# One contiguous token range per core, each with its own branch of the program

## The reference

```python
u = rmsnorm(h, ln1_g); z = u @ w_in       # -> zb, zc, zv (1024 each), q_lat 768, kv_lat 512, k_rope 64, gates 4096
y_conv = (zb * causal_dwconv3(zc * zv, conv_w)) @ w_conv_out
q = (rmsnorm(q_lat) @ w_q_b)              # 16 heads of 192
kv = (rmsnorm(kv_lat) @ w_kv_b)           # 16 heads of 128 (k) + 128 (v)
# per head: RMS norm of q and k over 192, rotary on the last 64, causal softmax(q k^T / sqrt(192)) v
y_mla = attention @ w_mla_out
h = h + (sigmoid(gate_a) * y_conv + sigmoid(gate_b) * y_mla) @ w_o
u = rmsnorm(h, ln2_g)
a = causal_dwconv3(u @ w_ffn_up, ffn_conv_w) + ffn_conv_b          # 2 * 5632 wide
h = h + (silu(a_gate) * a_up) @ w_ffn_down
```

## Time and profile before

| | us |
|---|---|
| median of 3 runs | 2585.52 |
| lowest, highest | 2583.54, 2963.02 |
| span of the profiled execution (slowest core, 0) | 2586.2 |
| spans of the 8 cores | 2577.1 to 2586.2 |
| PE busy | 2530.2 |
| DVE busy | 1483.1 |
| ACT busy | 1031.8 |
| POOL busy | 184.1 |
| HBM read | 320.30 MB |

### The profile page before, as it was taken

How to read it: one execution, slowest core, us unless ns; L and a number is a source line. 1 busy time by engine, 2 the same in 40 slices (tenths; PEclk the granted TensorE clock), 3 DMA queues, 4 the chain that set the end, 5 groups by cost and what they waited for, 6 DMA issues and landing times.

```text
span 2586.2 us, 51956 instructions; the slowest of 8 cores (2577.1 to 2586.2 us)
## 1 busy us (share of the span) xinstructions
PE 2530.2 (98%) x18360; PEld 1640.8 (63%) x18360; DVE 1483.1 (57%) x3020; ACT 1031.8 (40%) x2044; POOL 184.1 (7%) x321
## 2 busy tenths in 40 slices
PE   4999999999999999999999999999999999999999
PEld 2887666666666666666666666666556646666544
DVE  3881788787877878751211122377547736777611
ACT  4883688888888888841111113300000000000000
POOL 1010000000000000000000000010111010111010
PEclk9999999999999999999999999999999999999999
DMA  9684111202020102334444466344444454444465
GB/s 195 165 140 76 23 37 23 43 19 48 14 49 21 40 13 44 105 78 78 70 81 72 73 142 146 67 75 78 68 82 74 70 82 79 74 75 75 85 131 118
DMA packets 64779, 195.69 MB, mean 76 GB/s; under 512 B 7248, under 2 KB 8784, under 8 KB 63440
## 3 DMA queue, kind: packets, MB, share of 16 engines
q0 software_dynamic: 45648, 144.33, 34.1%
q1 hardware_dynamic: 18880, 48.03, 5.9%
HBM read 320.30 MB, written 15.83 MB: 130 GB/s over the span
## 4 chain that ended last, share of the span: by engine, by line
PE 95%; DMA 2%; DVE 2%; issue 1%; ACT 1%; SPq 0%; DVEq 0%; POOL 0%; ACTq 0%; POOLq 0%
PE ps L516 95%; DMA arena<-wkvin 1%; DVE arena L530 1%; DVE arena L534 1%; ACT arena L523 1%; DMA arena<-xg 1%; SPq L550 0%; DVE arena L540 0%; DVEq L200 0%; DVE arena L547 0%; POOL arena L550 0%; ACTq L200 0%; POOLq L200 0%; SPq L200 0%
## 5 line engine op out<-in xcount | busy, mean ns | idle before, releaser
L516 PE MATMUL ps<-arena 128*128 128x390 bf16 (+9 forms) x18360 | 2530.2, 300 | 53.2 <-ACT arena L523 25.1
L516 PEld LDWEIGHTS ps<-arena 128*128 128x128 bf16 x18360 | 1640.8, 98 | 942.3 <-issue 82.5
L534 DVE TENSOR_TENSOR arena<-ps,arena 128x390 f32<-128x390 f32 (+6 forms) x713 | 353.8, 502 | 812.7 <-PE ps L516 787.2
L534 DVE TENSOR_TENSOR arena<-arena 128x130 bf16<-128x130 bf16 (+18 forms) x1522 | 663.7, 474 | 231.8 <-ACT arena L523 204.3
L523 ACT ACTIVATE arena<-ps,arena 128x260 bf16<-128x260 f32 (+7 forms) x992 | 518.9, 546 | 419.0 <-PE ps L516 363.3
L523 ACT ACTIVATE arena<-arena 128x390 bf16<-128x390 f32 (+14 forms) x412 | 269.0, 677 | 844.6 <-DVE arena L530 725.3
L530 DVE SCALAR_TENSOR_TENSOR arena<-arena 128x1024 f32<-128x1024 f32 (+9 forms) x499 | 371.7, 762 | 37.1 <-ACT arena L523 13.1
L523 ACT ACTIVATE arena<-ps 128x512 bf16<-128x512 f32 (+11 forms) x635 | 319.8, 524 | 112.9 <-PE ps L516 107.1
L550 POOL DMA_DIRECT2D arena<-wall x286 | 167.1, 585 | 2235.5 <-PE ps L516 2181.8
L543 DVE TENSOR_SCALAR arena<-arena 128x1024 f32<-128x1024 f32 (+1 forms) x90 | 72.3, 803 | 0.0
L530 DVE SCALAR_TENSOR_TENSOR arena<-ps,arena 128x256 bf16<-128x256 f32 (+1 forms) x80 | 33.2, 464 | 6.7 <-ACT arena L523 4.1
(11 more groups left out here) (3 smaller groups left out, 0.3 us busy)
## 6 DMA issues: line engine op xcount, KB each, us to landing
arena<-wall POOLq DMA_DIRECT2D x182, 512.0 KB, 5.3
arena<-wall POOLq DMA_DIRECT2D x64, 352.0 KB, 4.7
arena<-xg POOLq DMA_DIRECT2D x22, 512.0 KB, 11.0
arena<-xo SPq DMA_DIRECT2D x16, 520.0 KB, 24.2
arena<-xg SPq DMA_DIRECT2D x8, 1024.0 KB, 6.5
arena<-wall POOLq DMA_DIRECT2D x32, 256.0 KB, 5.0
outT<-arena SPq DMA_DIRECT2D x31, 256.0 KB, 3.4
arena<-wkvin SPq DMA_DIRECT2D x16, 320.0 KB, 16.3
```

The source lines that it names most:

```text
L516: S.add(PE, lambda e: e.matmul(out, lhsT=lhsT, rhs=rhs, start=start, stop=stop), reads, writes, cost=max(width(rhs) / 2400.0, 0.055) + 0.003)
L534: S.add(DVE, lambda e: e.tensor_tensor(out=out, in0=in0, in1=in1, op=op), reads, writes, cost=dcost(out, in0, in1) + held)
```

## The change

Core j of a batch element owns one contiguous range of tokens, `BOUNDS` = 0, 1238, 2304, 3246, 4096. The program now has four bodies, one per range, made by `share_program(Share(j), ...)`; each engine reads `which` from DRAM and takes its body in one of four `If`s. A body handles keys only up to its range's end (`nkb` = 10, 18, 26, 32 key blocks). It has `na` = n + 2 columns in chunks of at most 510 (3 chunks on the first two ranges, 2 on the others). Each range's queries are cut in chunks of at most 512 (3, 3, 2, 2), each chunk's key blocks begin at the column where the block becomes visible, and one PSUM bank (4 or 5) holds a chunk's result; the mask is one triangle of 128 columns. Six `PT` buffers instead of four, `LA` 4 instead of 2, four `acc`. `b0_units`, `halo`, `halo2` go; the halo tokens come with the block that holds them. In the first stage own blocks may be both of a group; on range 0 the first two groups are own blocks that come as bf16 for `latents` and again as f32, late, for `own`. Attention and conv results are loaded for the mix ahead of the last score only where they lie under the rotary keys. `up` does both weights per chunk and its conv steps per chunk; the FFN's down groups are 10, 10, 10, 7, 7 tiles instead of 4 x 11, and its last groups use chunks `O` of at most 512.

```diff
+BOUNDS = (0, 1238, 2304, 3246, 4096)
+class Share:
+    def __init__(self, j):
+        self.s, self.e = BOUNDS[j], BOUNDS[j + 1]
+        self.n = self.e - self.s
+        self.na, self.nu = self.n + 2, self.n + 4
+        self.t0 = self.s - 2
+        self.h0 = 2 if self.first else 0
+        self.nkb = 2 * ((self.e + 255) // 256)
+        self.nkh = (self.e + 127) // 128
+        self.k = 128 * self.nkb
+        self.T = split(self.na, 510)
+        self.chunks = [(self.h0 + o, self.h0 + o + n) for o, n in split(self.na - self.h0, 512)]
+        self.O = split(self.n, 512)
...
+def emit(nc, which, progs):
...
+    def body(e, eng):
+        v = eng.value_load(which[0:1, 0:1])
+        for j, (S, final_waits) in enumerate(progs):
+            with eng.If(v == j):
+                S.replay(e, eng, eng_sem, chan_sem, final_waits)
...
     def oload(i, behind=()):
-        dma(SP, xo_[i % 3].rearrange("p k n -> p (k n)"), xg[i * 512:i * 512 + 128, :], ...)
+        b = sh.own[i][0]
+        dma(SP, xo_[i % 3].rearrange("p k n -> p (k n)"), xg[b * 128:b * 128 + 128, :], ...)
...
     def own(i):
+        b, g, h, _ = sh.own[i]
+        lo, hi = max(128 * b, sh.s - 4, 0), min(128 * b + 128, sh.e)
+        o = lo - (sh.s - 4)
+        x0, n = lo - 128 * b, hi - lo
         for k in range(16):
-            stt(u_own[:, k, o:o + 128], xo_[i % 3][:, k, :], C("g1", k), rstdx[:, y, 0:128], ALU.mult, ALU.mult,
+            stt(u_own[:, k, o:o + n], xo_[i % 3][:, k, x0:x0 + n], C("g1", k), rstdx[:, y, 128 * h + x0:128 * h + x0 + n],
+                ALU.mult, ALU.mult,
...
+    for h in range(NH):
+        for ci, (c0, c1) in enumerate(sh.chunks):
+            kbs = [kb for kb in range(sh.nkh) if 128 * kb <= sh.t0 + c1 - 1]
+            cs = h * len(sh.chunks) + ci
+            span[cs] = (len(pieces), len(pieces) + len(kbs))
+            for kb in kbs:
+                pieces.append((cs, h, kb, max(c0, 128 * kb - sh.t0), c0, c1))
...
-    NPT = 4
-    PT, TPT = P4.slabs(NPT, [912], BF16, "PT")
-    acc, Tacc = P4.slabs(2, [912], F32, "acc")
+    NPT = 6
+    PT, TPT = P4.slabs(NPT, [sh.CW], BF16, "PT")
+    acc, Tacc = P4.slabs(4, [sh.CW], F32, "acc")
...
+    def pv(i):
+        cs, h, kb, a, c0, c1 = pieces[i]
+        b = 4 + cs % 2
+        mm(PS[b][:, a - c0:c1 - c0], Vh[hb][:, kb, :], PT[:, x, a - c0:c1 - c0], i == span[cs][0], i == span[cs][1] - 1,
...
-                if (tag, i) in mixed or Tsrc[i].w is None or (tag == "gc" and i == 7 and st_s.units):
+                if (tag, i) in mixed or Tsrc[i].w is None or (st_s.units and t[i].hi > kro):
...
     def up(j):
+        for t, (off, n) in enumerate(T3):
+            for gi, key, A__, y_, Ty_, jc in ((0, "fg", Ag, yg, Tyg, j), (1, "fu", Au, yu, Tyu, 44 + j)):
+                for k in range(16):
+                    mm(PS[p][:, 0:n], w[:, k, :], u2[:, k, off:off + n], k == 0, k == 15, [Tw, Tu2[k]], [TP[p]])
+                tt(A__[:, off:off + n], PS[p][:, 0:n], rstd2[:, t, 0:n], ALU.mult, ...)
+                ts(y, A__[:, lo + 2:lo + 2 + m], C("fcw", 3 * jc + 2), C("fcb", jc), ALU.mult, ALU.add, rd, [Ty_[x]])
+                stt(y, A__[:, lo + 1:lo + 1 + m], C("fcw", 3 * jc + 1), y, ALU.mult, ALU.add, ...)
+                stt(y, A__[:, lo:lo + m], C("fcw", 3 * jc + 0), y, ALU.mult, ALU.add, ...)
```

More of the change, by code:

```diff
@@ new lines, in emit, with _ @@
+def emit(nc, which, progs):
+    for S, _ in progs:
+        S.finalize()
+    eng_sem = {e: nc.alloc_semaphore("sem_" + e) for e in ENGS}
+    chans = []
+    for S, _ in progs:
+        chans += [c for c in S.chan_cnt if c not in chans]
+    chan_sem = {c: nc.alloc_semaphore("dsem_" + str(c)) for c in chans}
+    def body(e, eng):
[3 more added lines that the diff above has]
+                S.replay(e, eng, eng_sem, chan_sem, final_waits)
+    with nc.Block() as block:
+        @block.tensor
+        def _(eng):
+            body(PE, eng)
+        @block.scalar
+        def _(eng):
+            body(ACT, eng)
+        @block.vector
+        def _(eng):
+            body(DVE, eng)
+        @block.gpsimd
+        def _(eng):
+            body(POOL, eng)
+        @block.sync
+        def _(eng):
+            body(SP, eng)
@@ L359, with split @@
+def split(n, most):
+    k = -(-n // most)
+    w = 2 * (-(-n // (2 * k)))
+    out, o = [], 0
+    while o < n:
+        out.append((o, min(w, n - o)))
+        o += w
+    return out
 QSCALE = 192.0 ** -0.5
 KB = 1024
-ARENA = 208896
+ARENA = 212800
 _c = {}
@@ L371 @@
 NC_CONST = _o
-T3 = [(0, 390), (390, 390), (780, 260)]
-T3C = [(0, 390), (390, 390), (780, 276)]
-HALF = 456
+FG = (10, 10, 10, 7, 7)
+FO = tuple(sum(FG[:g]) for g in range(6))
+NFT = 14
 def weight_plan():
@@ L984, in build_program, with ownof, loaded @@
+    def ownof(g):
+        return max([i for i, o in enumerate(sh.own) if o[1] == g] + [-1])
+    def loaded(g, h):
+        return at("cast") >= mode[(g, h)] if (g, h) in mode else at("ld%d" % g) > 0
+    rlast, rprior = {}, {}
+    for g in range(NG):
+        rprior[g] = ownof(rlast[rslab[g]]) if rslab[g] in rlast else -1
+        rlast[rslab[g]] = g
+    for g in range(NG):
         if g == 1:
@@ new lines, in plain, with sums @@
+    def plain(cs):
+        a, b = span[cs]
+        return b - a >= 4 and all(pieces[a + m][3] == pieces[a + m][4] for m in range(4))
+    def sums(i):
+        cs, h, kb, a, c0, c1 = pieces[i]
+        x, m = i % NPT, i - span[cs][0]
+        n = c1 - c0
+        A = a - c0
+        y = 2 * (cs % 2)
+        xp = (i - 1) % NPT
+        if plain(cs):
+            if m < 4:
+                if m % 2:
+                    z = y + m // 2
+                    tt(acc[:, z, 0:n], PT[:, xp, 0:n], PT[:, x, 0:n], ALU.add, [TPT[xp], TPT[x]], [Tacc[z]])
+                return
+            z = y + m % 2
+            tt(acc[:, z, A:n], acc[:, z, A:n], PT[:, x, A:n], ALU.add, [Tacc[z], TPT[x]], [Tacc[z]])
+        elif m == 0:
+            cp(acc[:, y, 0:n], PT[:, x, 0:n], [TPT[x]], [Tacc[y]])
+        else:
+            tt(acc[:, y, A:n], acc[:, y, A:n], PT[:, x, A:n], ALU.add, [Tacc[y], TPT[x]], [Tacc[y]])
```

975 lines of the change are left out of this document (448 added, 527 removed).

## The result

The changed kernel takes 2486.74 us (median, 2485.44 to 2486.83); against the kernel before the ratio is 0.9618, with a 95% interval of 0.9601 to 0.9635. It is 3.8% faster; the forecast of 2444 us meant 5.5%.

What follows compares the result with a forecast made beforehand. PE's columns bound the kernel; slowest type 0: start 143 + heads 543.0 + 24.7 + behind them 1694.0 + 29.5 + tail 2.8 = 2437.0, plus branches 8: span 2445, median 2444 us; range 2400 to 2500, its own 2428 to 2464.

Steps and rivals of the forecast that it cites:

- Bound and columns: Whole kernel: PE's columns set the time; they fall from 2448.7 us to 2264.7 to 2284.0, a gain of 165 to 182.
- Start of type 0: First stage, first range: ends at 143 us (120 to 155), set by DVE's own products and a chain of buffer reloads.
- The rival at 20%, start hidden: First stage, type 0: own blocks done by 100 to 120 us, type 1 or 0 last at 2400 to 2425; 20%.
- the q latents read it whole: First stage: it ends only when every own block is in `u_own`, since the query latents read all of it.
- Feed-forward part costed at nothing: Feed-forward: three short conv steps per chunk replace one of 1024; fixed costs add a fifth at most, charged 0 us.
- Branches: Reading `which` and testing it four times, leaping over up to three foreign programs: 8 us, between 0 and 25.
- Four at about 2: Branches: four leaps at about 2 us each, nearest to the shortest DMA landing of 1.7 us, making the 8 us.
- the upper bound of 25: Branches: one register read and four leaps at 5 us, three times the shortest DMA landing, 25 us at most.
- Losses in the heads: Head stage: 6.2 ns lost per matmul beside the columns, 24.7, 37.2, 38.2 and 45.4 us on types 0 to 3.
- Head chain on type 3: Head stage: rival that pieces form a dependent chain and type 3 is last, 2498 to 2546, mild form 2450 to 2500; 14%.
- Code loading: Whole program: rival that instruction blocks aren't fetched ahead after a leap, 269 us for 251 packets, giving 2713 us; 3%.
- Weights and mix loads at nothing: Weight DMAs (share 0.48 to 0.59 on type 3) and later mix loads stay covered: 0 us, mix at most 14.

Runs made afterwards that it cites:

- own_nogain: Changed kernel with each own block's 16 products made one product over all slabs, gain g1 left out; 2472.13 us in one execution.
- ffn_wide: Changed kernel with feed-forward taps, silu and product run once over the whole range again, first multiply still per chunk; 2469.83 us, ratio 0.9546.
- ffn_inter: Changed kernel with gate and up convolution steps taking turns on DVE, each chunk's product issued behind the next chunk's first two products; 2469.52 us, ratio 0.9543.
- before_chunked: Kernel before, with only the feed-forward convolution, silu and product run per chunk of one PSUM bank; 2668.65 us, ratio 1.0312.
- nested_rev: Changed kernel with branches as an if/else-if chain, type 3 tested first, type 0 last; types 0 to 3 ended at 2486.0, 2480.2, 2396.2, 2400.3 us (cores 4-7).
- one_type1: Changed kernel holding only type 1's body, without branch or type read, run by all eight cores; median span 2469.7 us.

## Why the prediction was right or wrong

**Bound and columns: right.** PE's columns set the time; the stage columns came out as counted, and the matmuls but for 14 behind the heads. The columns fell by 165 to 184 us (the prediction's own sums give 184 for type 3, not 182). On types 2 and 3 they fell by 180 and 184, and the spans by 187 and 169.

**Start of type 0: right mechanism, and the number partly by luck.** Forecast 143, measured 142.2 (137.1 on core 4), with PE idle ahead of it and DVE as its last releaser; own_nogain shows the chain. The rival at 20%, start hidden, falls. But the steps differ from those forecast. DVE's products on type 0, the first, the fifth block and the last three blocks (start, us):

```profile
71.05 0.34 DVE L599 SCALAR_TENSOR_TENSOR arena<-arena 128x128 bf16<-128x128 f32 x1
...
116.88 2.71 DVE L599 SCALAR_TENSOR_TENSOR arena<-arena 128x128 bf16<-128x128 f32 x10 [5.18 <-ACT arena L592]
...
133.34 13.58 DVE L599 SCALAR_TENSOR_TENSOR arena<-arena 128x128 bf16<-128x128 f32 x50 [2.17 <-DMA arena<-xg]
```

They began at 71, not 80; `own(4)` began at 116.9 for 118; the last block ran from 141.8 to 146 us and not from 138 to 143. PE started at 142.2 all the same, because the first query latent matmul needs only the first slab of that block: "the q latents read it whole" was wrong as a condition for the start. An early first step, slower reloads and an early PE cancelled out. What the forecast didn't see either is the landing of head weights, 11.4 us of PE's wait on type 0 and 7.0 on type 1: hidden by the own chain on the one, while on the other it makes 7.0 of the +9.3 in the heads.

**Feed-forward part costed at nothing: wrong, and the largest miss.** This is the step of the prediction that failed: a term put at nothing. It read "the three short conv steps per chunk replace one of 1024; DVE is busy 539 of 925.6 us now, and fixed costs add a fifth at most". Three things were wrong in it. It took the share of the whole stage, where a chunk is the unit that counts: nine DVE steps in 5.43 us against 4.99 us of matmuls on type 1. It added only busy time, and too little of that (720.0 us for 580.6 with wide steps, a quarter more): a dependent step also has 0.1 us of hole ahead of it, which no busy row shows. And it was reckoned for no width, though a chunk of 356 gives PE less time to hide the same fixed cost than one of 472. In its place the runs showed DVE as the bound of a narrow chunk, at 49 to 54 us on type 1 (ffn_wide, ffn_inter), of which some 8 are the slower clock that goes with the waits; before_chunked shows the same part at +80 us on the kernel before. Without it type 1 would have ended at 2436, 17 us above its forecast.

**Branches: mis-sized and misplaced.** 8 us stood for every type. Measured: 1.5 us for the read of the type (first DMA 2.55 for 1.07), 5.0 us for each leap ahead, 4.0 for each behind. That is 13.4 us on type 0 (all but 1.5 behind the last matmul, 11.9 of 15.2 less 3.3), 12.8 on type 1 (5.6 + 7.2), and 16.5 ahead of the body on type 3, whose first stage ended 16.5 us late. "Four at about 2" counted four leaps where each type takes three, at half the price; the upper bound of 25 held. That the 16.5 us agree with the lateness on type 3 is chance: with no leap ahead of it that stage ended at 204.8 (nested_rev), 4.5 us before its forecast, and three leaps moved it by 23.

**Losses in the heads: mis-sized by the wrong unit.** I spread 48.2 us over 7752 matmuls. After, types 0 to 3 lose 44.0, 46.5, 37.1 and 44.9 us with 3986, 6002, 6156 and 7324 matmuls (type 1 with its 7.0 us for weights), so the loss doesn't go by matmuls. On type 0 this is +19 us, on type 3 nothing. PE on type 0 is idle for 20.6 us in them (28.7 less the 8.1 just ahead of the first matmul), against 9.5 us on type 3, and 8.8 of the 20.6 lie between 260 and 320 us. Why the loss lies between 37 and 47 us on all types wasn't tried and stays open.

**Head chain on type 3: falls.** Its heads took 995.6 us, forecast 996.1, with ACT busy 796.85 and DVE 719.91 of 995 us (80% and 72%, forecast 81% and 75%). A slip in the sum didn't matter: the rows give 1.04 ns a column and 0.15 us fixed for DVE's sums, where it took 1.06 and 0.13, and so +178 us instead of +170.

**Code loading: falls** in the form of the rival: one_type1 and the four-bodied program take the same time inside the body. Its price of 269 us was too high by its own rows, which give 1.07 us for the 154 packets of q8 and some 0.4 for the 97 of q14, 206 us in all. **Weights and mix loads at nothing: right** within what was seen: the gates and the mix lost 4.8 to 8.8 us on the four types, and waits for weights behind the heads sum to under 2 us on types 2 and 3.

On the slowest core the errors are +50 for DVE in the feed-forward part, +9 in the heads and +4.5 at the start. The forecast named type 0 as the last, by 30 to 50 us, and types 2 and 3 within 10 us of each other; type 1 was the last, and types 2 and 3 were 17 to 18 us apart. With the wide convolution type 0 is the last, at 2470. That the measured time lies within the wide range of 2400 to 2500 is luck: the range was made wide for rivals that all fell, and the forecast's own range, 2428 to 2464, was missed.

## What to carry to other kernels

Cost a vector engine per chunk and not per stage: count its steps, each with its fixed cost and its width, and add a hole of some 0.1 us for each step that reads the step before. Compare the sum with the matmul time of that same chunk, at its narrowest. A busy share of 86% was full here. Let independent steps take turns, or make them wide, and if cores run different bodies behind branches, count a few us for each body that is leapt over on either side, and place the longest-running type where it leaps least.
